# A decoder layer on one core: 62 depthwise-convolution taps from VectorE to ScalarE and GpSimd, and the key norms' inverse roots from GpSimd to ScalarE

## The reference, cut to what matters

```python
glu = a * jax.nn.sigmoid(g)
xc = jnp.concatenate([conv_state, glu], axis=1)
y = conv(xc, conv_w[:, None, :], groups=CONV_CH) + conv_b     # causal, width 31
y = jax.nn.silu(layer_norm(y, conv_ln_g, conv_ln_b))
```

```python
k_nope = (ckv @ w_uk).reshape(..., N_HEADS, NOPE_DIM)
k_nope = k_nope * rsqrt(mean(k_nope ** 2, axis=-1) + EPS) * g
sc = q_nope . k_nope + q_pe . k_pe            # then softmax over all pages, and the sum of the latents
```

## Time and profile before

| what | value |
|---|---|
| device time, three runs | 1678.46, 1680.36, 1681.87 us (median 1680.36) |
| span of the profiled execution | 1678.9 us; no time of its own is given beside the span, which lies within the three runs |
| PE busy | 1647.5 us (98%) |
| DVE busy | 1228.8 us (73%) |
| ACT busy | 666.2 us (40%) |
| POOL busy | 527.1 us (31%) |

### The profile page before, as it was taken

How to read it: one execution, slowest core, us unless ns; L and a number is a source line. 1 busy time by engine, 2 the same in 40 slices (tenths; PEclk the granted TensorE clock), 3 DMA queues, 4 the chain that set the end, 5 groups by cost and what they waited for, 6 DMA issues and landing times.

```text
span 1678.9 us, 28976 instructions
## 1 busy us (share of the span) xinstructions
PE 1647.5 (98%) x10683; PEld 1482.3 (88%) x10683; DVE 1228.8 (73%) x1843; ACT 666.2 (40%) x1248; POOL 527.1 (31%) x343
## 2 busy tenths in 40 slices
PE   8999999999999999999989999999999999999998
PEld 8999888777999999878879999999999888888886
DVE  5486876777999999866798777777776676954544
ACT  5302366765544444743443222222222335442111
POOL 2303695321656656621233222222221000700000
PEclk9999999999999999999999999999999999999999
DMA  6401000001332222230205444444444877661101
GB/s 199 146 1 50 15 1 0 2 22 38 115 106 60 62 67 73 61 107 1 76 26 178 146 145 145 145 144 143 144 143 149 290 269 242 194 222 67 48 30 47
DMA packets 156045, 172.89 MB, mean 103 GB/s; under 512 B 35155, under 2 KB 107376, under 8 KB 155805
## 3 DMA queue, kind: packets, MB, share of 16 engines
q1 hardware_dynamic: 153939, 170.52, 31.5%
q10 hardware_dynamic: 2002, 1.03, 0.2%
HBM read 131.06 MB, written 40.80 MB: 102 GB/s over the span
## 4 chain that ended last, share of the span: by engine, by line
PE 81%; DVE 12%; issue 3%; POOL 2%; ACT 1%; SPq 1%; DMA 0%; ACTq 0%; DVEq 0%; POOLq 0%
PE ps L2656 22%; PE ps L2658 21%; PE ps L2657 21%; DVE arena L2218 2%; DVE arena L1810 2%; PE ps L3114 1%; PE ps L2936 1%; PE ps L2909 1%; PE ps L2889 1%; PE ps L627 1%; PE ps L2662 1%; PE ps L2663 1%; POOL stats L987 1%; PE ps L2893 1%; PE ps L2999 1%
## 5 line engine op out<-in xcount | busy, mean ns | idle before, releaser
L1138 POOL TENSOR_TENSOR arena<-arena,mhalf 128x32 f32<-128x32 f32 (+1 forms) x40 | 180.6, 4521 | 114.3 <-DVE arena L2223 114.3
L2656 PE MATMUL ps<-cw_hi,pT_hi 128*128 128x288 f32 x512 | 163.9, 320 | 0.9 <-DVE pT_lo L2109 0.8
L1810 DVE SCALAR_TENSOR_TENSOR arena<-arena,tapw 128x1024 f32<-128x1024 f32 x120 | 159.7, 1330 | 1.8
L2430 DVE TENSOR_TENSOR dn_lo<-dn_raw,dn_hi 128x1024 fp32r<-128x1024 f32 x83 | 115.5, 1401 | 61.3 <-ACT dn_hi L1713 60.6
L2656 PE MATMUL ps<-T_hi,S_hi 128*128 128x272 f32 x528 | 152.7, 289 | 3.6 <-DVE F_B_r L681 1.8
L2657 PE MATMUL ps<-F_B_r,S_hi 128*128 128x272 f32 x528 | 152.3, 288 | 0.0
L2658 PE MATMUL ps<-T_hi,S_lo 128*128 128x272 f32 x528 | 151.9, 288 | 0.0
L2657 PE MATMUL ps<-cw_lo,pT_hi 128*128 128x288 f32 x512 | 150.8, 294 | 0.0
L2658 PE MATMUL ps<-cw_hi,pT_lo 128*128 128x288 f32 x512 | 150.7, 294 | 0.0
L1713 ACT ACTIVATE dn_hi<-dn_raw 128x1024 fp32r<-128x1024 f32 x83 | 87.6, 1060 | 130.8 <-DMA dn_raw<-wt_mid 61.8
L2656 PE MATMUL ps<-dn_hi 128*128 128x512 f32 x308 | 120.2, 390 | 0.2 <-DVE U L2348 0.2
(11 more groups left out here) (416 smaller groups left out, 4823.2 us busy)
## 6 DMA issues: line engine op xcount, KB each, us to landing
dn_raw<-act_mid SPq DMA_DIRECT2D x77, 256.0 KB, 2.8
arena<-in_cache_ckv SPq DMA_DIRECT2D x128, 128.0 KB, 2.0
dn_raw<-in_w_down SPq DMA_DIRECT2D x45, 256.0 KB, 3.6
w_raw<-in_w_gate SPq DMA_DIRECT2D x22, 512.0 KB, 4.0
w_raw<-in_w_up SPq DMA_DIRECT2D x22, 512.0 KB, 5.3
arena<-in_w_down SPq DMA_DIRECT2D x22, 512.0 KB, 6.0
act_mid<-arena SPq DMA_DIRECT2D x11, 1024.0 KB, 7.8
wt_mid<-arena SPq DMA_DIRECT2D x11, 1024.0 KB, 4.4
```

Of the source, the lines that this page charges most:

```text
L1138: nc.gpsimd.tensor_tensor(rstd_k[:, g0:g1, :], ms_k[:, g0:g1, :], mhalf[:, 0:(g1 - g0) * NH].rearrange("p (g h) -> p g h", h=NH), ALU.pow) ...
L1810: ins = nc.vector.scalar_tensor_tensor(y_of(c), glu[:, c, k:k + SEQ], tapw[:, c, k:k + 1], y_of(c), ALU.mult, ALU.add)
L2430: nc.vector.tensor_tensor(dn_lo_r[s], dn_raw[s], dn_hi[s][0], ALU.subtract).then_inc(s_("a_split"), 1)
L2656: mm(out, left[0], right[0], start=start, stop=False)
```

## The change

The last two of the convolution's four chunks of channels (62 taps, `LATE_TAPS`) leave DVE. ACT makes each product of a window of `glu` and the tap's column of weights (`late_scale`, 128x1024, the chunk's first tap straight into `y_of(c)` with the bias); POOL adds it to the sum (`late_add`, 60 additions of 128x1024). Products lie in two buffers in turn (`tap_prod`), so ACT waits for the addition two before. They are placed behind `page_square` on pages 0, 2, 3, 4, 6, 8, 10, 11, 12 and 14, ten in a sequence, from page 6 of the first sequence to page 8 of the seventh. DVE keeps 62 taps, the last 3 on pages 0 to 2 of the first sequence.

The inverse roots of sequences 0 to 6 are made by ACT (`page_root`: Ln with the eps as bias, then Exp with scale -0.5, 128x32 each, four a sequence, on pages 5, 9, 13 and page 1 of the next); DVE's scale-and-eps and POOL's power go for those. The last sequence keeps both as before. One table set with both functions is loaded ahead of the attention stage in the place of an Exp.

The semaphores `ys_prod` and `ys_summed` are renamed `conv_products` and `conv_sums` and go on counting in this stage. PE waits for `self_place` 5 ahead of the first `lat_T`.

```diff
-NSTAT = len(STAT_PAGES)
+NSTAT = 4
+LATE_CHUNKS = 2
+LATE_TAPS = [(c, k) for c in range(CCH - LATE_CHUNKS, CCH) for k in range(CK)]
+LATE_PAGES, LATE_SKIP = (0, 2, 3, 4, 6, 8, 10, 11, 12, 14), 4
...
+        tap_prod = Region(NT * DM).take(2, SEQ)
+
+        def late_added(i):
+            return (CK - 2) * (i // CK) + min(i % CK, CK - 2)
...
-            for b in range(NSEQ):
-                for q, (g0, g1) in enumerate(STAT_PAGES):
-                    pool.wait_ge(s_("msk_ready"), NSTAT * b + q + 1)
-                    nc.gpsimd.tensor_tensor(rstd_k[:, g0:g1, :], ms_k[:, g0:g1, :],
-                                            mhalf[:, 0:(g1 - g0) * NH].rearrange("p (g h) -> p g h", h=NH), ALU.pow).then_inc(s_("rstdk_ready"), 1)
-                    if q == 0 and 1 <= b < NSEQ - 1:
-                        low_q(b + 1)
...
+            def late_add(i):
+                c, k = LATE_TAPS[i]
+                pool.wait_ge(s_("conv_products"), 4 * CCH + i + 1)
+                if k >= 2:
+                    pool.wait_ge(s_("conv_sums"), 4 * CCH + late_added(i - 1))
+                add = nc.gpsimd.tensor_tensor(y_of(c), y_of(c), tap_prod[:, i % 2, :], ALU.add)
+                add.then_inc(s_("conv_sums" if k < CK - 1 else "y_ready_c"), 1)
...
+            for b in range(NSEQ - 1):
+                late_adds(b, 0, 3)
+                if b >= 1:
+                    low_q(b + 1)
+                late_adds(b, 3, len(LATE_PAGES))
+            for q, (g0, g1) in enumerate(STAT_PAGES):
+                pool.wait_ge(s_("msk_ready"), q + 1)
+                nc.gpsimd.tensor_tensor(rstd_k[:, g0:g1, :], ms_k[:, g0:g1, :],
+                                        mhalf[:, 0:(g1 - g0) * NH].rearrange("p (g h) -> p g h", h=NH), ALU.pow).then_inc(s_("rstdk_ready"), 1)
...
-            nc.scalar.activation(unit_out[:, 1:2], ident[0:1, 0:1], ACT.Exp)
+            nc.scalar.preload_act_table_set("natural_log_exp_and_others")
...
+            def page_root(b, q):
+                act.wait_ge(s_("ksum_done"), NPAGE * b + 4 * q + 4)
+                part = rstd_k[:, 4 * q:4 * q + 4, :]
+                ch.link(nc.scalar.activation(part, ms_k[:, 4 * q:4 * q + 4, :], ACT.Ln, bias=eps_n[:, 0:1]))
+                nc.scalar.activation(part, part, ACT.Exp, scale=-0.5).then_inc(s_("rstdk_ready"), 1)
+
+            def late_scale(i):
+                c, k = LATE_TAPS[i]
+                if k == 0:
+                    act.wait_ge(s_("y_ready_c"), c)
+                    bias = gcol[:, c + COLS["conv_b"][0]:c + COLS["conv_b"][0] + 1]
+                    nc.scalar.activation(y_of(c), glu[:, c, 0:SEQ], ACT.Identity, scale=tapw[:, c, 0:1], bias=bias).then_inc(s_("conv_products"), 1)
+                    return
+                if k >= 2 and late_added(i - 2) > 0:
+                    act.wait_ge(s_("conv_sums"), 4 * CCH + late_added(i - 2))
+                nc.scalar.activation(tap_prod[:, i % 2, :], glu[:, c, k:k + SEQ], ACT.Copy, scale=tapw[:, c, k:k + 1]).then_inc(s_("conv_products"), 1)
...
                     page_square(b, g)
+                    if b < NSEQ - 1 and g in (5, 9, 13):
+                        page_root(b, (g - 5) // 4)
+                    if b >= 1 and g == 1:
+                        page_root(b - 1, 3)
+                    if g in LATE_PAGES and 0 <= len(LATE_PAGES) * b + LATE_PAGES.index(g) - LATE_SKIP < len(LATE_TAPS):
+                        late_scale(len(LATE_PAGES) * b + LATE_PAGES.index(g) - LATE_SKIP)
...
-            tap_list = iter([(c, k) for c in range(CCH) for k in range(CK)])
+            tap_list = iter([(c, k) for c in range(CCH - LATE_CHUNKS) for k in range(CK)])
...
-                        if g == g1 - 1:
+                        if b == NSEQ - 1 and g == g1 - 1:
```

More of the change, by code:

```diff
@@ L1025, in taps_sample @@
                 if i >= 1:
-                    pool.wait_ge(s_("ys_summed"), i)
+                    pool.wait_ge(s_("conv_sums"), i)
                 g = glu_s[:, c, b0:b0 + YQ, 0:TQ]
@@ L1029, in taps_sample @@
                 w = tapw[:, c, :].unsqueeze(1).unsqueeze(1).to_broadcast([P, YQ, TQ, CK])
-                nc.gpsimd.tensor_tensor(prod, rows, w, ALU.mult).then_inc(s_("ys_prod"), 1)
+                nc.gpsimd.tensor_tensor(prod, rows, w, ALU.mult).then_inc(s_("conv_products"), 1)
             for t in range(NT):
@@ L1064, in set_page @@
                 pool.wait_ge(s_("page_set"), s + 1)
-            pool.wait_ge(s_("ys_prod"), 4 * CCH)
+            pool.wait_ge(s_("conv_products"), 4 * CCH)
             nc.gpsimd.memset(s_self[64:P, :, :, :], NEG).then_inc(s_("self_place"), 1)
@@ L1133, in last_sum, with late_adds @@
                 weight_sum("S4", s)
-            for b in range(NSEQ):
-                for q, (g0, g1) in enumerate(STAT_PAGES):
-                    pool.wait_ge(s_("msk_ready"), NSTAT * b + q + 1)
-                    nc.gpsimd.tensor_tensor(rstd_k[:, g0:g1, :], ms_k[:, g0:g1, :],
-                                            mhalf[:, 0:(g1 - g0) * NH].rearrange("p (g h) -> p g h", h=NH), ALU.pow).then_inc(s_("rstdk_ready"), 1)
-                    if q == 0 and 1 <= b < NSEQ - 1:
-                        low_q(b + 1)
[L1142 to L1145, removed]
+            def late_add(i):
[5 more added lines that the diff above has]
+                add.then_inc(s_("conv_sums" if k < CK - 1 else "y_ready_c"), 1)
+            def late_adds(b, first, last):
+                for i in range(max(len(LATE_PAGES) * b + first - LATE_SKIP, 0), min(len(LATE_PAGES) * b + last - LATE_SKIP, len(LATE_TAPS))):
+                    if LATE_TAPS[i][1] > 0:
+                        late_add(i)
+            for b in range(NSEQ - 1):
[7 more added lines that the diff above has]
+                                        mhalf[:, 0:(g1 - g0) * NH].rearrange("p (g h) -> p g h", h=NH), ALU.pow).then_inc(s_("rstdk_ready"), 1)
+                if q == 0:
+                    ln_pool(1, P)
+                if q == 1:
+                    mix_pool(1, P)
             ln_pool(2, P)
@@ L1818, in sum_sample @@
                 c, b0 = i // 4, (i % 4) * YQ
-                dve.wait_ge(s_("ys_prod"), i + 1)
+                dve.wait_ge(s_("conv_products"), i + 1)
                 out = y_s[:, c, b0:b0 + YQ, :]
                 ch.link(nc.vector.reduce_sum(out, prod, AXX))
-                nc.vector.tensor_scalar(out, out, gcol[:, c + COLS["conv_b"][0]:c + COLS["conv_b"][0] + 1], None, ALU.add).then_inc(s_("ys_summed"), 1)
+                nc.vector.tensor_scalar(out, out, gcol[:, c + COLS["conv_b"][0]:c + COLS["conv_b"][0] + 1], None, ALU.add).then_inc(s_("conv_sums"), 1)
             dve.wait_ge(s_("g_mix_loaded"), 16)
@@ L2091, in quad @@
             def quad(b, s, q):
-                dve.wait_ge(s_("rstdk_ready"), NSTAT * b + (q + 1 if q < 3 else NSTAT))
+                dve.wait_ge(s_("rstdk_ready"), NSTAT * b + (q + 1 if q < 3 or b < NSEQ - 1 else len(STAT_PAGES)))
                 dve.wait_ge(s_("sc_done"), 4 * b + q + 1)
@@ L3117, in lat_T @@
             def lat_T(b):
+                if b == 0:
+                    pe.wait_ge(s_("self_place"), 5)
                 pe.wait_ge(s_("olat_ready"), b + 1)
@@ L3124, in _ @@
             chunk_T(-1, 0)
-            pe.wait_ge(s_("ys_summed"), 4 * CCH)
+            pe.wait_ge(s_("conv_sums"), 4 * CCH)
             pe.wait_ge(s_("o_evac"), NH)
```

## The result

The changed kernel takes 1721.91 us (median of 4 runs, 1717.62 to 1724.57) against 1681.11 before (4 runs), a ratio of 1.0242 with a 95% interval of 1.0227 to 1.0256: slower by 41 us.

What follows compares the result with a forecast made beforehand. PE was taken to set the stage's pace, with DVE just in time behind it. Freed taps -1, ACT 0, holds +26 and page 12 +3 gave +28 us, so 1680.4 + 28 = 1708 us; 8-in-10 range 1683 to 1726.

Steps and rivals of the forecast that it cites:

- What bounds the kernel: In the stage of the cached sequences PE sets the pace, with DVE just in time behind it.
- The chain's 8.8% for the taps: Share of the stage that the chain of waits gives the tap line L1810; the prediction held it shows no time lost.
- The gain taken as 1 us: What PE gains in the stage from DVE losing 62 taps: 0 to 4 us, taken as 1.
- Roots and ACT's load: ACT comes to 31 of 37 us a sequence with products and roots, not the bound; taken 0, bound 5 us.
- The rival of ACT as the bound: Additions harmless, PE waits for ACT on page 7, 0.5 to 1 us in each of six sequences: 1685 us, chance 0.06.
- that of table loads: Rival: a table load on ACT at each change between Ln and Exp: 1712 us, chance 0.03.
- The holds: On pages 2 to 4 POOL's additions hold DVE's instructions ahead of PE's `max_T`: 26 us, bounds 7 and 32.
- The worked line of events: Fourth sequence, pages 2 to 4: page 2's addition starts 0.3 us ahead of L2141; three additions in line delay L2108 5.3 us.
- The fork named for the other order: On page 2 L2141 starts before the addition; PE then stands 3.4 us at `max_T`.
- The fork without the copy: The copy L2148 ahead of the maximum is not held; the two orders then give 2.9 and 1.2 us.
- the clock: Behind each of six PE holes, 3.4 us at half pace, 1.7 us each; bounds 0 and 10, taken 0.
- Page 12: Additions of pages 10 to 12 may hold L2126, making `low_pair` late: 0 to 1.3 us in five sequences, 3 us taken.

Runs made afterwards that it cites:

- e1_no_adds: Changed kernel with GpSimd's 60 additions each replaced by a memset of one column, ACT's products and roots kept: 1681.21 us, ratio 1.0000 to the kernel before.
- e3_other_pages: Changed kernel with the ten products a sequence on other pages, none on pages 2 and 3: 1681.20 us, ratio 1.0000 to the kernel before.
- e8_max_ready: Changed kernel with no products on pages 2 and 3, and the maximum over twelve blocks on page 0 instead of 1: 1679.29 us, ratio 0.9994.
- e2_roots_only: Changed kernel with only the inverse roots moved to ACT, all 124 taps staying on VectorE: 1681.17 us, ratio 0.9999 to the kernel before.
- e7_later_root: Changed kernel with the last four pages' root on page 2 instead of 1, so page 2's product comes 0.45 us later: 1706.86 us, ratio 1.0155.
- e4_copy_early: Changed kernel with the copy L2148 made on page 15 of its own sequence, not between last quad and maximum: 1702.61 us, ratio 1.0119.
- e6_half_adds: Changed kernel with each GpSimd addition made as two of 512 columns: 1694.16 us, ratio 1.0082 to the kernel before.
- e12_one_memset: Changed kernel with each GpSimd addition replaced by a memset of 128x1024, which reads nothing: 1680.63 us, ratio 0.9998 to the kernel before.

## Why the prediction was right, and which terms were off

**What bounds the kernel** was read rightly. PE's even steps of 0.13 us said that the stage belongs to PE and that VectorE's 35 of 37 busy us cost nothing; e1_no_adds and e3_other_pages free VectorE of all 62 taps and gain 0, and e8_max_ready is 1.2 us under the kernel before, within its interval. The chain's 8.8% for the taps were worth nothing. The gain taken as 1 us is 0 to 1.

**Roots and ACT's load** at 0: right (e2_roots_only, e1_no_adds). The rival of ACT as the bound falls with e1_no_adds, that of table loads with e2_roots_only. A root took 0.56 us against 0.55 taken.

**The holds** stood as argued from the earlier trace rows: L2141, then the copy, then L2108, each until the end of one addition. The worked line of events gave 5.3 us for the order that came true, in the fourth sequence. There PE idled 4.47 us, because the additions took 2.00 us and not the 2.3 of the working; in the fifth, with additions of 2.3 to 2.4, it idled 5.55. With the clock kept up the pair of pages grew by 5.4 us in three sequences and by 4.4 in the three whose additions are shorter. The fork named for the other order (3.4 us) is what e7_later_root shows, 19.8 us over seven waits of which six are long. The fork without the copy (2.9 us) is e4_copy_early, 16.5 us. Taken was the middle of two orders, 4.3 us by six, 26 us; measured without the clock 29. That these are so near is partly luck: only the first order came true, for which the working had 32 us, and the shorter additions in three sequences took off the difference.

**The mis-sized term is the clock.** The prediction named it, took 0 and bounded it at 1.7 us a hole, 10 us, by the one stretch of 3.4 us in the earlier trace rows. The runs show 12 us in the stage, above that bound. Two steps failed. A zero was taken for want of a row, where a hole of 2.04 us had already shown the effect. And the bound took every stretch to be 3.4 us long, as at the end of the last sequence, but four of the six were of 6.8 us, as the one in the fifth sequence above. The forecast's 28 us became 41: 29 for the holes and 12 for the clock. The 3 us put on page 12, which did not come, stood against a part of that, so the sum is nearer than its terms.

**Page 12** was taken at 3 us for five sequences. In the changed kernel L2126 was held in two, for 1.93 and 1.92 us, and took 0.16 to 0.20 in the others, where it fell between two additions or beside none. Its cost is 0: in each of these sequences the pair of pages 14 and 15 takes what it took before, within 0.1 us (4.4 us, or 5.9 to 6.0 where a chunk is transposed too), and so does the pair after it. So even where the hold came, the instructions between it and PE's next wait had more slack than the working gave them; no run separates where that slack comes from. `quad` on page 15, said to fall between additions, was held too, to 1.30 and 1.38 us in two sequences, and that cost nothing either.

## What to carry to other kernels

Before work goes from VectorE to GpSimd, look in the trace for the records of VectorE instructions with two SBUF inputs that would overlap a GpSimd instruction reading SBUF, and of short copies from SBUF to SBUF that would overlap one that reads or only writes it, and then for the VectorE instruction whose result PE waits for with no slack: it is the length and the place of each GpSimd instruction that cost, not the sum. An engine that is busy 95% just behind PE is not the bound as long as PE's starts are evenly spaced. And a hole in PE's work costs more than its length, since the products behind it may run at half clock.

## What the runs showed of the hardware that was not expected

- Each of the six holes of 4.5 to 5.6 us in PE's work brought 3.4 or 6.8 us at half clock and a loss of 1.4 to 2.8 us; needless products in it took away the loss (1723.6 to 1708.7 us). Shorter holes brought it only at times: in e6_half_adds two of the three of 2.1 us and none of the three of 1.5 us.
- Writing alone does not hold two-input instructions: beside a memset of GpSimd they took their usual 0.42 and 0.23 us, beside an addition up to 2.44 and 1.97. It does hold a short copy: 0.85 to 0.89 us against 0.22 (L2113 in e12_one_memset).
- GpSimd's power does not hold either: in the kernel before, 35 taps ran wholly inside a power's record (L1138), and each took its usual 1.27 to 1.28 us. So what brought the holds is not that GpSimd works beside VectorE, but what it does there.
- Additions of one form took 2.00 us on the third chunk and 2.3 to 2.4 on the fourth. On pages 2 to 4 the third chunk is worked on in sequences 1 to 3 (numbered from 0), the fourth in 4 to 6, and so three records there grew from 2.00, 1.54 and 1.63 us (L2141, L2148, L2108) to 2.43, 1.89 and 1.97, and the hole from 4.5 to 5.5. What makes the difference between the additions was not tried.
